# Main-half normalisation by scaling a feature-major copy of x, and a beginning that takes the values first, in a RetNet/Mamba-2 hybrid layer on eight cores

## The reference

```
h = x + mixer(rmsnorm(x, norm_mix_w)) ; y = rmsnorm(h + mlp(rmsnorm(h, norm_mlp_w)), norm_final_w)

def rmsnorm(x, w): return x * rsqrt(mean(x*x, axis=-1) + 1e-6) * w

def mixer(h):
    q, k, v, g | z, xBC, dt = split(h @ w_in)          # 4 retention heads of 256, 16 SSD heads of 64
    retention: rope(q), rope(k); chunks of 128; state = decay * state + k^T v; y = norm(y) * silu(g)
    SSD: xBC = silu(conv4(xBC)); dt = softplus(dt + bias); chunked scan with state 128; gated norm with silu(z)
    return concat(y_ret, y_ssd) @ w_out
def mlp(h): return relu(h @ w_up)**2 @ w_down           # 2048 -> 8192 -> 2048
```

## Time and profile before

| | before |
|---|---|
| median of 3 runs | 1742.88 us (1741.87 to 1743.29) |
| the profiled execution, its own time | 1744.06 us |
| its span (slowest core, core 5) | 1742.5 us; the 8 cores 1732.3 to 1742.5 |
| PE (TensorE) busy | 1668.5 us, 96% |
| DVE (VectorE), ACT (ScalarE) busy | 697.6 us, 40%; 406.5 us, 23% |
| DMA | 155 MB written, 89 GB/s mean |

### The profile page before, as it was taken

How to read it: one execution, slowest core, us unless ns; L and a number is a source line. 1 busy time by engine, 2 the same in 40 slices (tenths; PEclk the granted TensorE clock), 3 DMA queues, 4 the chain that set the end, 5 groups by cost and what they waited for, 6 DMA issues and landing times.

```text
span 1742.5 us, 26674 instructions; the slowest of 8 cores (1732.3 to 1742.5 us)
## 1 busy us (share of the span) xinstructions
PE 1668.5 (96%) x10410; PEld 968.8 (56%) x10410; DVE 697.6 (40%) x1295; ACT 406.5 (23%) x767; POOL 60.6 (3%) x118
## 2 busy tenths in 40 slices
PE   1789999999999999999999999999999999999997
PEld 1678887766657677644444444444444444444443
DVE  1365765667766555536622121221121221212225
ACT  3333322567652222202211000110001100011013
POOL 0000000000000000000000000000000000000000
PEclk9899999999999999999999999999999999999999
DMA  9727436042326513752554325443244433444424
GB/s 203 213 56 138 113 74 107 4 74 50 74 53 142 97 32 67 122 170 49 97 97 73 73 54 102 83 76 70 52 97 78 82 64 67 97 73 76 85 58 169
DMA packets 23307, 155.13 MB, mean 89 GB/s; under 512 B 2704, under 2 KB 2960, under 8 KB 5904
## 3 DMA queue, kind: packets, MB, share of 16 engines
q0 software_dynamic: 16416, 116.10, 37.1%
q1 hardware_dynamic: 6768, 37.33, 6.3%
HBM read 261.13 MB, written 8.39 MB: 155 GB/s over the span
## 4 chain that ended last, share of the span: by engine, by line
PE 92%; DMA 3%; DVE 1%; issue 1%; ACT 1%; another core or an unknown queue 1%; SPq 0%; DVEq 0%; ACTq 0%; POOLq 0%
PE psum L452 90%; PE psum L455 2%; DMA arena<-xp 2%; DMA arena<-w_ret 2%; ACT arena L473 1%; DVE arena L480 1%; DVE arena L489 0%; SPq L442 0%; DVE arena L484 0%; ACT L473 0%; DVEq L311 0%; DVEq L330 0%; ACTq L330 0%; POOLq L330 0%
## 5 line engine op out<-in xcount | busy, mean ns | idle before, releaser
L452 PE MATMUL psum<-arena 128*128 128x512 bf16 (+6 forms) x9674 | 1635.3, 331 | 23.2 <-DVE arena L480 13.9
L452 PEld LDWEIGHTS psum<-arena 128*128 128x128 bf16 (+1 forms) x9674 | 921.6, 99 | 714.1 <-issue 29.8
L480 DVE TENSOR_TENSOR arena<-arena 128x512 bf16<-128x512 f32 (+6 forms) x351 | 190.7, 550 | 379.6 <-ACT arena L473 370.9
L473 ACT ACTIVATE arena<-psum 128x512 f32<-128x512 f32 (+3 forms) x234 | 130.6, 565 | 786.2 <-PE psum L452 767.1
L480 DVE TENSOR_TENSOR arena<-arena,psum 128x512 f32<-128x512 f32 x190 | 130.0, 687 | 368.1 <-PE psum L452 367.7
L473 ACT ACTIVATE arena<-arena 128x512 bf16<-128x512 f32 (+3 forms) x211 | 158.8, 766 | 412.0 <-DVE arena L489 170.0
L480 DVE TENSOR_TENSOR arena<-psum,arena 128x512 f32<-128x512 f32 (+4 forms) x250 | 174.9, 730 | 159.2 <-PE psum L452 138.0
L489 DVE SCALAR_TENSOR_TENSOR arena<-psum,arena 128x512 f32<-128x512 f32 (+1 forms) x164 | 112.6, 695 | 49.7 <-ACT arena L473 38.5
L473 ACT ACTIVATE arena<-psum,arena 128x128 f32<-128x128 f32 (+3 forms) x212 | 91.4, 508 | 120.2 <-PE psum L452 98.7
L455 PE MATMUL psum<-arena 128*128 128x128 bf16 x736 | 59.3, 228 | 42.1 <-DVE arena L484 36.6
L455 PEld LDWEIGHTS psum<-arena 128*128 128x128 bf16 x736 | 50.9, 103 | 50.3 <-issue 43.6
(11 more groups left out here) (15 smaller groups left out, 15.6 us busy)
## 6 DMA issues: line engine op xcount, KB each, us to landing
arena<-w_up POOLq DMA_DIRECT2D x32, 1024.0 KB, 10.1
arena<-w_down POOLq DMA_DIRECT2D x32, 1024.0 KB, 8.6
arena<-w_ret POOLq DMA_DIRECT2D x22, 1024.0 KB, 10.1
arena<-xm SPq DMA_DIRECT2D x16, 1024.0 KB, 9.0
arena<-xp SPq DMA_DIRECT2D x8, 1024.0 KB, 39.5
arena<-w_xs POOLq DMA_DIRECT2D x8, 1024.0 KB, 10.5
arena<-w_out POOLq DMA_DIRECT2D x8, 1024.0 KB, 10.1
y<-arena SPq DMA_DIRECT2D x14, 512.0 KB, 3.2
```

What stands on the lines that cost most here:

```text
L452: P.op("pe", lambda e: e.matmul(R(out), lhsT=lhsT, rhs=rhs, start=start, stop=stop), [lhsT, rhs], [out], c, lat=163.0)
L473: P.op("act", lambda e: e.activation(out=R(out), in_=R(in_), func=func, **kw), ins, outs, c, lat=0.0, table=table)
L480: P.op(eng, lambda e: e.tensor_tensor(out=R(out), in0=R(a), in1=R(b), op=op), [a, b], [out], dcost(out, True), lat=0.0)
```

## The change

- **The normalisation of `xm`.** The host also gives a feature-major copy, `xmt`, of shape (2, 4, 128, 2048): half hf (512 rows), group g (4 blocks of 128 features), features on partitions, 4 x 512 columns. `square_m(c)` loads a chunk of `xm` into `xbuf[0]`, squares and sums it on ScalarE; `root_m(hf)` takes the 4 roots at once (`newton` on 4 columns) and spreads them over the partitions by 4 float32 products of 128 columns with the identity, into a PSUM bank; `scale_m(hf, g)` makes 4 products of 512 columns on VectorE, xmt times weight times that bank, into `xnM`, and then loads the next group into the same buffer `xbuf[1]`. The 128 transposes, the 16 copies of 1024 columns and the 8 scalings of 2048 columns of `norm_m` are gone; 8 loads of 1 MB are new.
- **The beginning.** Values first: `v0` and `pv1` are the first two weights, then `pb0`, `px00`, `pk0`, `pk1`. In the loop over chunks stand the values of heads 0 and 1 and the first convolutions; all keys come later (`keyP`). `identb` is a copy made by VectorE from the float32 identity, which moved into the first constants (320 columns). The chunks 1 to 5 of `xp` are issued at once; rope tables and the other constants come after chunk 7.
- **The middle.** `v0_chunk` of the main half, `dtM` and `prod(0)` are woven into the long stretch (at 0.03 to 0.85, 0.9, and 0.9 to 1.0 of it). The load of `SEL` is issued after it. The 16 small products for `dgh` and `dgl` follow.
- **The planner's model of transfers.** Two queues that share 330 bytes/ns as 1 to 1.4, with 1.5 or 4 us to start and 1.5 us to land, in place of one line.

```diff
+DMA_SHARE = {"sp": 1.0, "pool": 1.4}
+DMA_START = {"sp": 1500.0, "pool": 4000.0}
+DMA_LAND = 1500.0
...
     need("v0", w_v0, [16, 272])
-    need("pk0", w_ret[0], [16, 256])
-    for what in ("pb0", "pk1", "pv1", "px00", "px01", "pk2", "pv2", "pb1", "px10", "pk3", "pv3", "px11"):
+    for what in ("pv1", "pb0", "px00", "pk0", "pk1", "px01", "pk2", "pv2", "pb1", "px10", "pk3", "pv3", "px11"):
...
     xl = [load_x(0, xp, xst[0])]
-    dma("pool", CB[:, 0:128], cstb[:, 0:128])
+    feed(2)
     dma("sp", CST[:, 0:C_SMALL], cst[:, 0:C_SMALL])
...
+    for c in range(1, 6):
+        xl.append(load_x(c, xp, xst[c]))
+    cp(identb, ident)
...
-        if c == 2 or c == 3:
+        if c < 4:
             feed(1, [xl[c]])
-        if c == 3:
+        if c == 2:
+            dma("sp", p_cos.rearrange("p a b -> p (a b)"), rope_p[:, 0, :])
+            dma("sp", p_sin.rearrange("p a b -> p (a b)"), rope_p[:, 1, :])
             dma("sp", CST[:, C_SMALL:C_END], cst[:, C_SMALL:C_END])
-        if c == 4 or c == 5:
-            load_x(c - 4, xm, xs_)
+        if c == 4:
+            load_x(0, xm, xs_)
+        if c == 5:
+            load_xt(0, 0)
...
-    def norm_m(c):
-        norm_front(xbuf[c % 2], xb[c % 2])
-        if c + 2 < 8:
-            load_x(c + 2, xm, xbuf[c % 2])
-        transpose16(xb[c % 2], nw, lambda hf: xnM[:, hf * 8:hf * 8 + 8, 4 + c * 128:132 + c * 128], "T")
-        if c == 0:
+    def square_m(c):
+        act(xb[0], xbuf[0], AF.Square, scale=2048.0 ** -0.5, accum=ssm[c // 4][:, c % 4:c % 4 + 1])
+        if c < 7:
+            load_x(c + 1, xm, xbuf[0])
+    def root_m(hf):
+        r = newton(ssm[hf], EPS, 4)
+        p = bank("T")
+        for k in range(4):
+            mm(p[:, k * 128:(k + 1) * 128], r[:, k:k + 1].to_broadcast([128, 128]), ident, True, True)
+        rowr[hf] = p
+    def scale_m(hf, g):
+        src = xbuf[1].rearrange("p (k t) -> p k t", k=4)
+        for k in range(4):
+            dc = g * 4 + k
+            stt(xnM[:, dc, 4 + hf * 512:516 + hf * 512], src[:, k, :], nw[:, dc:dc + 1], rowr[hf], ALU.mult, ALU.mult)
+        if (hf, g) != (1, 3):
+            load_xt(hf + (g + 1) // 4, (g + 1) % 4)
+        if hf == 0 and g == 3:
             cp(xnM[:, :, 0:4], xnP[:, :, 1024:1028])
...
+    weave((rest, 0.0, 0.95), (group0[5:] + ssdP(1), 0.0, 0.85), (main_in, 0.03, 0.85),
+          ([dtM], 0.9, 0.9), (prod(0), 0.9, 1.0))
+    dma("pool", SEL.rearrange("p h n -> p (h n)"), cstb[:, B_SEL:B_END])
```

More of the change, by code:

```diff
@@ L203, in schedule, with event @@
         free = {e: 0.0 for e in self.ENG}
-        chan = 0.0
+        dq = {"sp": [], "pool": []}
+        dnow = [0.0]
+        def event(q, now):
+            live = [k for k in q if q[k] and q[k][0][2] <= now]
+            rate = {k: DMA_RATE * DMA_SHARE[k] / sum(DMA_SHARE[x] for x in live) for k in live}
+            times = [now + q[k][0][0] / rate[k] for k in live]
+            times += [q[k][0][2] for k in q if q[k] and q[k][0][2] > now]
+            if not times:
+                return None
+            t = min(times)
+            done = None
+            for k in live:
+                q[k][0][0] -= rate[k] * (t - now)
+                if q[k][0][0] <= 1e-3 and done is None:
+                    done = q[k].pop(0)[1]
+            return t, done
@@ new lines, in landing, with settle @@
+        def landing():
+            q = {k: [list(x) for x in dq[k][:3]] for k in dq}
+            now = dnow[0]
+            while True:
+                got = event(q, now)
+                if got is None:
+                    return None
+                now = got[0]
+                if got[1] is not None:
+                    return now + DMA_LAND
+        def settle(i):
+            for s in succ[i]:
+                se = recs[s]["eng"]
+                same = se == recs[i]["eng"] and not recs[i]["dma"]
+                at = beg[i] + recs[i]["cost"] if same and se == "pe" else fin[i] + XLAT[se]
+                rtime[s] = max(rtime[s], at)
+                indeg[s] -= 1
+                if indeg[s] == 0:
+                    ready[se].append(s)
@@ new lines, in advance @@
+        def advance(limit, one):
+            while True:
+                q = {k: [list(x) for x in dq[k]] for k in dq}
+                got = event(q, dnow[0])
+                if got is None or got[0] > limit:
+                    if got is not None and limit > dnow[0]:
+                        live = [k for k in dq if dq[k] and dq[k][0][2] <= dnow[0]]
+                        for k in live:
+                            dq[k][0][0] -= DMA_RATE * DMA_SHARE[k] / sum(DMA_SHARE[x] for x in live) * (limit - dnow[0])
+                    dnow[0] = max(dnow[0], limit) if limit < 1e17 else dnow[0]
+                    return
+                dq.update(q)
+                dnow[0] = got[0]
+                if got[1] is not None:
+                    fin[got[1]] = got[0] + DMA_LAND
+                    settle(got[1])
+                    if one:
+                        return
@@ L235, in schedule @@
                     best = (k[0], e, k[1])
+            land = landing()
+            if land is not None and (best is None or land < best[0]):
+                advance(1e18, True)
+                continue
             st, e, i = best
@@ L270, in schedule @@
                         freeat[k] = max(fin[x] + XLAT["pe"] for x in self.vops[v])
[L271 to L277, removed]
+            if not r["dma"]:
+                settle(i)
+        while landing() is not None:
+            advance(1e18, True)
         self.sim_ns = max(fin)
@@ L600, in build_program @@
             need(f"d{fb}{k}", w_down[fb * 8 + k], [8, 512])
-    ssr = Ring(list(range(24)))
+    ssr = Ring(list(range(20)))
     nwr = Ring(list(range(8)))
@@ L901, in build_program @@
     assert off[0] <= pos_e
-    spot(pos_t)
-    acrep = alloc([8, 96], F32)
-    for c in range(8):
-        v0_chunk(xnM, c, lambda src, c=c: act(v0m[:, c, :], src, AF.Copy))
-    release("v0")
     def dtM():
```

99 lines of the change are left out of this document (50 added, 49 removed).

## The result

| | before | changed |
|---|---|---|
| median | 1743.09 us (1741.87 to 1743.78, 4 runs) | 1721.78 us (1718.77 to 1723.3, 4 runs) |
| ratio | | 0.9876, 95% interval 0.9859 to 0.9894 |
| span of the profiled execution | 1742.5 us | 1720.2 us (core 2; the 8 cores 1713.5 to 1720.2) |

Faster by 21.3 us, where 29 were forecast.

A forecast was written before the change was run, and what follows sets the result against it. PE, busy 96% of the span, was taken as the bound, plus a late beginning and three holes. Terms -5.5 - 17 - 6.5 - 7.5 + 7 = -29.5 us gave 1714 us against 1742.88, range 1701 to 1731.

The forecast's parts named there:

- Term 1: PE's own work: 128 transposes of the main norm gone, 8 small float32 products new; -5.5 us, bounds -4 to -5.5.
- Term 2: The beginning: first product near 28 us, last transposes of `xp` near 76; -17 us, bounds -12 to -22.
- Terms 3 and 4: Waits for `w_ret` weights gone, -6.5 us (-4 to -7); waits around `dtM`'s 22 products covered, -7.5 us (-3 to -9).
- Term 5: New single-buffered loads: squares hidden, scalings stall PE before the main half's values; +7 us, bounds 0 to +18.
- C: Rival, `dtM` not covered: its inputs come later than planned and the holes stay, 7 us; 1721 us, chance 10%.
- A: Rival at the beginning: x does not land earlier, so the beginning gains only 6 us; 1725 us, chance 14%.
- B: Rival: the single buffers decide, three uncovered reloads in each half at 16.2 us; 1760 us, slower; chance 5%.
- D: Rival: removed transposes cost more than back to back, 0.6 us more per batch, half the new loads' cost missing; 1702, 6%.

The follow-up runs named there:

- e14: Changed kernel with weight loads `pk2` and `px10` held until reloads of `xm` and `xmt` landed, and separate buffers for the convolutions' sums: 1710.23 and 1710.06 us.
- e12: Changed kernel, but with the old main norm `norm_m`, its transposes and its two buffers, woven into the new middle: 1710.5 us, ratio 0.9811.
- e6: Kernel before the change with only the planner's new model of transfers (`DMA_SHARE`, `DMA_START`, `DMA_LAND`): 1731.1 us, ratio 0.9933.
- e1: Changed kernel's new beginning and planner, with the old `norm_m` and the unwoven middle put back: 1722.4 us, ratio 0.9896.
- e5: Changed kernel with every instruction in place, but reloads of `xm` and `xmt` bring 16 of 2048 columns (output invalid): 1712.3 us, ratio 0.9831.
- e7: Changed kernel with weight loads held back: `pk2` until chunk 3 of `xm` landed, `px10` until the fourth group of `xmt` landed: 1712.9 us, ratio 0.9823.
- e9: Changed kernel with separate buffers for the convolutions' sums, before shared with the rotation of keys; squares written in place: 1721.04 us, ratio 0.987.
- e15: e14 with the scalings woven in singly and over more of the long stretch, the main values after them: 1735.33 us, one run.
- e8: Changed kernel with two buffers for the squares of `xm`, written in place: 1723.3 us, ratio 0.9881.
- e11: e7 with the two buffers for the squares of e8: 1720.16 and 1719.85 us, ratio 0.9865.

## Why the prediction came out as it did

The sign and the chain of reasons held, and terms 1 to 4 came out near their sizes. Term 5 was mis-sized, +7 for +16, and that is the gap between 1714 and 1721.8. The other misses partly cancel: term 2 fell 2.8 us short, terms 3 and 4 gave 2.1 more.

**Term 1 (-5.5): held, indirectly.** PE's busy time fell by 8.6 us, but that counts modelled ends and the clock. Better is what is left of the profiled core's span without its loss up to 400 us. That is 1667 to 1669 us in the four kernels with the transposes and 1659 to 1665 in the ten with the scaling, on average 7 us less. Single pairs scatter (4.5 us for e14 against e12, 8 for the changed kernel against the one before), so 5.5 is not told from 8. The estimate by the Trainium skill ("TensorE: Matmul & The Clock Gate", Part 4: PE-mode transpose), 275 ns a transpose, would have made it 34 us. The runs go with the row of 56 ns.

**Term 2 (-17): measured -14.2** (55.6 to 41.4 us of loss up to 116), -15.5 in e12. First product at 28.88 against 28, but the last transposes ended at 82.7, not 76. ScalarE's square of the last chunk stood at 72.62 and its transposes at 81.61, 9.0 us where the prediction had counted 4.0 from landing to transposes: copies of products, for which ScalarE waits, and a table load of 1.28 us stand between. The prediction took PE's order as it stood and did not ask which edit makes it. It wrote off the planner's orders elsewhere as differing "by a few rows only". The planner's model alone gives 8.4 of the 14.2 (e6), and the new order of weights, loads and values the rest.

**Terms 3 and 4 (-14 together): measured -16.1,** just beyond their bounds of -7 to -16: the loss of 116 to 400 from 17.8 before to 1.7 in e12, where nothing of term 5 is mixed in. The weights' part was the planner's as well: 0.9 us of loss in 116 to 200 in e6. For `dtM` the test is e1 against e12, and 298:324 of the changed kernel, 26.00 busy: the cover by `prod(0)` was complete, where I had left 2 us.

**Term 5 (+7): measured +16,** the loss of 116 to 400 in the changed kernel (17.7) above e12 (1.7). The loss between 116 and 200 us is made up of 7.0 us of waits from 130 us on (0.97, 2.92 and 3.14), 3.63 us of wait ahead of that, and 5.5 us at a lower clock. The 7.0 are what the term had, 4 to 7 us for the scalings (and 2 in the second half, where none came). Two things it put at nothing. The first is the squares, "hidden, by 6 us": I compared the time at which the root is ready with the time at which PE wants it, as if the squares only fed the root. But a square that waits for its load also stops everything behind it on ScalarE, and PE's next transposes waited 3.63 us for that. The second is the clock: terms 3 and 4 count what the lower clock behind a hole costs, and term 5 does not. Beneath both, "7.2" us a reload, a median of spread loads, was taken for loads that now come in a burst beside weights: of the eight up to 180 us two took 16.3 and 17.0, as the one of the earlier trace rows had, and two took 11.8 and 12.4. The term's upper bound, +18 for "two of the six so slow", covers the result partly by luck: two loads were so slow, but e5 and e7 put only 8 to 9 of the 16 us on the reloads' duration.

The rest seems to lie in VectorE's order: with own sums for the convolutions beside the gate, 4 more are gone (e14 against e7, 8.0 to 4.0 of loss; 2.7 us of time). The same sums without the gate gained nothing clear (e9). What the last 4 hang on stays open, since e15, which removed them, changed the rest of the order too.

**Rivals.** C (1721) and A (1725) are nearest in their numbers, but by luck: C's holes at `dtM` are gone, and for A x did land earlier. B, the single buffers, was the right place, but it cost 9 us above the forecast and not 46. The Trainium skill ("Trainium Kernel Development and Optimization", Best Practices) says to double-buffer so that DMA and compute overlap. The old norm's two buffers did cover a load of 16.1 us in e12. The second buffer by itself did not shorten the time in e8 (1723.3) or with the gate in e11 (1720.0 against 1712.9), because the planner's order put the square of the slow reload ahead of work that PE needs, and it did help the cores whose reload was not slow. No run kept the order and changed the number of buffers alone. C did not happen. D can't be told from the scatter of term 1.

**A version that beats both.** e12 at 1710.5 us is 11.3 faster than the changed kernel and 33 faster than the one before, with 8 MB less of loads than the changed kernel. e14 equals it (1710.23 and 1710.06). The new norm is not what the change gained by: it gave back a third of what the rest brought.

## What to carry to other kernels

- Price a wait for a transfer by what stands behind it on the engine that works in order, not only by the consumer that it feeds, and add what the lower clock after the wait costs. Here the waits were 10.7 us and the clock 5.5 more.
- When a change bundles a new order with a new algorithm, run the square of the two. Here the algorithm saved some 5 to 8 us of TensorE's work and made 16 of holes, and the order hid it.
- Where loads of two queues collide, first try to hold back the one that has slack (8.9 us here for two dependencies).
- Look at the order that a second buffer brings with it. A planner that trusts the earlier load moves its consumer ahead of other work, and a load that is late all the same then costs more (9.92 us of wait in e8 against 3.63).

## What was not expected of the hardware

- The landing time of a 1 MB load on SP's queue depended on what POOL's queue had under way, more than on its own queue: 5.2 us at 83 us of the changed kernel and 5.4 at 138 us of e12, both alone; 8.5 (median) for two together in e8 with no weights; 11.3 beside `w_xs` in e7; 16.1 to 17.0 beside a `w_ret` and a `w_xs`; 16.8 and 21.7 for two in e8 beside the same.
- A hole often costs half to two thirds as much again by the clock, but not always. In 116 to 130 of the changed kernel 3.63 us of idle came with 0.24 x 10.37 = 2.5 us at a lower grant; up to 200 it was 10.7 of idle and 5.5 by the clock. In e9, 2.16 us of idle came with a grant of 0.88 there. But before, 3.2 us of idle in 200 to 230 came with a grant of 1.00. What decides it these runs do not show.
- An edit of the planner's constants and its simulation of transfers, with no operation changed, moved the time by 12 us (e6). On a kernel whose order is planned, the belief about transfers is a tuning knob of its own.
